# Result stores of the expert pairs issued by the sync engine instead of the scalar engine, from four result buffers

## The chip, the cores and the metric

The kernel runs on one core of a Trainium2 chip. The metric is device time in microseconds (us) of one execution. Five engines work beside each other and meet only at semaphores: TensorE (PE, matmuls and transposes into eight PSUM banks), VectorE (DVE), ScalarE (ACT), GpSimd (POOL) and the sync engine (SP). SP and ACT each issue DMAs into a queue of their own, q1 and q10 in the profile; sixteen DMA engines carry the packets of all queues.

## The reference

A block with attention, retention and a mixture of experts is followed by a second block of two layers. The change touches the experts alone. Of 64 experts every one of 512 tokens picks two; all is float32:

```python
def expert_block(args):
    xb, e = args
    hid = jax.nn.silu(xb @ w1[e]) * (xb @ w3[e])   # 1024 -> 512
    return hid @ w2[e]                             # 512 -> 1024

y_slots = lax.map(expert_block, (x_slots, blk_eid)).reshape(n_blocks * MOE_BLOCK, D)
y_assign = y_slots[dest].astype(jnp.float32) * s_gate[:, None]
return jax.ops.segment_sum(y_assign, s_tok, num_segments=T).astype(x2.dtype)
```

w1, w3 and w2 of an expert are 2 MB each, 403 MB in all; y_slots is an intermediate in DRAM.

## The kernel before

The kernel is a row of blocks: norm, mixer, merge, norm with the router's loads, the experts (`moe_block`), then `layers_block`, whose first work is to gather rows of `y_slots` with indirect DMAs. A block begins when all engines are through with the one before.

In `moe_block` each expert has 32 slots for tokens (CAP), and the experts go in pairs: 32 pairs, as eight iterations (`NIT`) of four pairs `pp`. Each engine runs its own loop over them.

*Weights.* A pair needs six loads of 2 MB, in the order w1, w3, w1, w3, w2, w2 (`PARTS`), each into one of eight slots `m.w` (`WSLOT`). `loads_of_router` issues the first eight ahead of the block. In `sp_moe`, SP then issues load x + 8 when the slot of load x is free: for the four up projection slots of a pair after `up_done`, for the two w2 slots after `down_done` (L1012 on). SP does nothing else here.

*PE* (`pair`): it waits for four loads, does the up projections of both experts into bank `pr` = pp % 2 (64 matmuls, L1068), raises `up_done`; for odd pairs it gathers the tokens of the next four experts (64 matmuls, L1053); then it waits for VectorE's `hid`, transposes it (L1077), waits for ACT's copy `ht`, for the two w2 loads, and for `yo_ready`, and does the down projection into bank 3 + pr (32 matmuls, L1087), `down_done`.

*ACT* (`act_moe`): Silu of the bank into `hs` (L1156), copy of gathered tokens for odd pairs (L1148), copy of the transposes (L1160). Then it waits for `yo_ready` and issues the store of the result (L1162): 128 partitions of 2 KB from `m.yo[pr]`, 256 KB, to `y_slots`, in a pattern whose outermost dimension is the half h of the columns, of size 2.

*VectorE* (`dve_moe`): the selection matrix for the next gather (L1293, L1310, L1315), the product `hid` (L1319), and the copy of the down projection from PSUM to `m.yo[pr]` (L1324), raising `yo_ready`. Before this copy it waits for `y_sent{pr}`, the store of the pair two before from the same buffer. In the order of VectorE's queue this copy stands ahead of the product of the next pair.

Semaphores y_sent0 and y_sent1 start at 16 (raised by ACT). At the end ACT waits for all stores. A last part for experts with more than 32 tokens (`sp.If(n > 0)`) follows on each engine.

Of the kernel before, what the change touches and what calls it, by code (L numbers as in the profile page):

```python
# [815 lines left out]
def merge_block(nc, m, G, banks, A):  # L816
    merge_memory(m)
    with nc.Block() as block:
# [81 lines left out]
        def _(pool):  # L900
# [8 lines left out]
CAP = 32  # L909
# [4 lines left out]
ROUTER_SEMS = ["rw_in", "logits_done", "logits_ready", "r_exp_in", "r_exp", "assigned", "counted",  # L914
               "routed", "zeroed", "eb_sent", "eb_in", "r_step"]
MOE_SEMS = ["up_done", "hs_ready", "hid_ready", "ht_turned", "ht_ready", "down_done", "yo_ready",
            "y_sent0", "y_sent1", "g_ready", "gather_done", "xt_ready", "g_step",
            "ov_in", "ov_g", "ov_gathered", "ov_xt", "ov_up", "ov_hs", "ov_hid", "ov_turned",
            "ov_ht", "ov_down", "ov_y", "ov_sent", "ov_step"] + [f"e_in{i}" for i in range(WSLOT)]
COMB_SEMS = [f"y_in{i}" for i in range(8)] + ["combined"]  # L920
# [2 lines left out]
def moe_memory(arena):  # L923
    m = persistent(arena)
    sp = Space(arena, m.free)
    m.hn = sp(T, D)
    m.rw = sp(KT, NG + NE)
    m.rb = sp(NG + NE)
    m.iota = sp(P)
    m.piota = sp(1)  # L930
    m.before, m.ones = sp(P), sp(P)
    m.lg = sp(T, NG + NE)
    m.r8 = [sp(T, 8) for _ in range(8)]
    m.r1 = [sp(T) for _ in range(12)]
    m.prod = sp(T, NG * GE)
    m.pick = [sp(T, NE) for _ in range(2)]
    m.both = sp(T, NE)
    m.pos = sp(T, NE)
    m.e64 = [sp(NE) for _ in range(5)]
    m.k8 = [sp(2, T) for _ in range(6)]  # L940
    m.yrel = sp(2, T)
    m.misc = sp(4)
    m.misc_i = sp(4).bitcast(i32)
    m.eb_i = sp(MORE).bitcast(i32)
    m.norm_at = sp.at
    m.G = sp(T, P)
    m.G1 = sp(T, P)
    m.xt = sp(KT, P)
    m.hs, m.hid = sp(FF), sp(FF)
    m.ht = sp(FF // P, 2 * CAP)  # L950
    m.yo = [sp(512) for _ in range(2)]
    at = sp.at
    m.w = [sp(KT * FF) for _ in range(WSLOT)]
    norm_views(m, m.norm_at)
    assert m.norm_smalls <= at
    return m
# [4 lines left out]
NGRP = NE // 4  # L961
# [17 lines left out]
def load_expert(sp, m, G, A, at, i):  # L979

    pp, j = at // 6, at % 6
    e = 8 * i + 2 * pp + (j // 2 if j < 4 else j - 4)
    sp.dma_start(m.w[at % WSLOT], expert_src(A, PARTS[j], e)).then_inc(G[f"e_in{at % WSLOT}"], 16)
# [16 lines left out]
        load_expert(sp, m, G, A, at, 0)  # L1000


def sp_moe(sp, m, G, A, eb_dram):
    sp.wait_ge(G["routed"], 1)
    sp.dma_start(eb_dram.rearrange("a b -> b a"), m.misc_i[0:MORE, 0:1]).then_inc(G["eb_sent"], 16)
    sp.wait_ge(G["eb_sent"], 16)
    sp.dma_start(m.eb_i[0:1, :], eb_dram).then_inc(G["eb_in"], 16)

    def loads(i, n):
        for x in range(n):  # L1010
            pp, j = x // 6, x % 6
            sp.wait_ge(G["up_done" if j < 4 else "down_done"], 4 * i + pp + 1)  # L1012
            load_expert(sp, m, G, A, x + WSLOT, i)

    with sp.Fori(0, NIT - 1) as i:
        loads(i, 24)
    loads(NIT - 1, 24 - WSLOT)
    sp.wait_ge(G["eb_in"], 16)
    n = sp.value_load(m.misc_i[0:1, 1:2], min_val=0, max_val=MORE - 1)
    with sp.If(n > 0):  # L1020
        sp.wait_ge(G["up_done"], NE // 2)
        sp.wait_ge(G["down_done"], NE // 2)
        with sp.Fori(0, n) as j:
            e = sp.value_load(m.eb_i[0:1, bass.ds(j, 1)], min_val=0, max_val=NE - 1)
            sp.wait_ge(G["ov_down"], j + 1)
            sp.dma_start(m.w[0], expert_src(A, "w1", e)).then_inc(G["ov_in"], 16)
            sp.dma_start(m.w[1], expert_src(A, "w3", e)).then_inc(G["ov_in"], 16)
            sp.dma_start(m.w[4], expert_src(A, "w2", e)).then_inc(G["ov_in"], 16)
# [105 lines left out]
def act_moe(act, m, G, banks, y_slots):  # L1134
    turned = banks[2][:, :].rearrange("p (f c) -> p f c", f=FF // P)
    act.wait_ge(G["r_exp_in"], 1)
    act.activation(m.r8[1], m.r8[0], ACT.Exp).then_inc(G["r_exp"], 1)
    act.wait_ge(G["r_exp_in"], 2)
    act.activation(m.r1[3], m.r1[2], ACT.Exp).then_inc(G["r_exp"], 1)

    act.sem_inc(G["y_sent0"], 16)
    act.sem_inc(G["y_sent1"], 16)
    act.sem_inc(G["ov_sent"], 16)

    def xt_copy(n):
        for d in range(2):
            act.wait_ge(G["gather_done"], n + d + 1)
            act.activation(m.xt[:, 4 * d:4 * d + 4, :],  # L1148
                           banks[5 + d][:, :].rearrange("p (a c) -> p a c", a=4), ACT.Copy)\
               .then_inc(G["xt_ready"], 1)  # L1150

    def experts(i, last):
        for pp in range(4):
            h, pr = pp // 2, pp % 2
            act.wait_ge(G["up_done"], 4 * i + pp + 1)
            act.activation(m.hs[64:128, :], banks[pr][0:64, :], ACT.Silu).then_inc(G["hs_ready"], 1)  # L1156
            if pr and not (last and h):
                xt_copy(4 * i + 2 * h + 2)
            act.wait_ge(G["ht_turned"], 4 * i + pp + 1)
            act.activation(m.ht, turned[:, :, 0:2 * CAP], ACT.Copy).then_inc(G["ht_ready"], 1)  # L1160
            act.wait_ge(G["yo_ready"], 4 * i + pp + 3)
            act.dma_start(y_slots[bass.ds(8 * CAP * i + 2 * CAP * pp, 2 * CAP), :]  # L1162
                          .rearrange("r (h c) -> h r c", h=2), m.yo[pr])\
               .then_inc(G[f"y_sent{pr}"], 16)

    xt_copy(0)
    with act.Fori(0, NIT - 1) as i:
        experts(i, False)
    experts(NIT - 1, True)
    act.wait_ge(G["y_sent0"], 16 * NGRP + 16)  # L1170
    act.wait_ge(G["y_sent1"], 16 * NGRP + 16)
    act.wait_ge(G["routed"], 1)
    n = act.value_load(m.misc_i[0:1, 1:2], min_val=0, max_val=MORE - 1)
    with act.If(n > 0):
        with act.Fori(0, n) as j:
            act.wait_ge(G["ov_gathered"], j + 1)
            act.activation(m.xt[:, :, 0:CAP],
                           banks[5][:, 0:KT * CAP].rearrange("p (a c) -> p a c", a=KT), ACT.Copy)\
               .then_inc(G["ov_xt"], 1)
            act.wait_ge(G["ov_up"], j + 1)  # L1180
            act.activation(m.hs[64:64 + CAP, :], banks[0][0:CAP, :], ACT.Silu).then_inc(G["ov_hs"], 1)
            act.wait_ge(G["ov_turned"], j + 1)
            act.activation(m.ht[:, :, 0:CAP],
                           turned[:, :, 0:CAP], ACT.Copy)\
               .then_inc(G["ov_ht"], 1)
            act.wait_ge(G["ov_y"], j + 1)
            act.dma_start(y_slots[bass.ds(CAP * (j + MAIN), CAP), :].rearrange("s (h c) -> h s c", h=2),
                          m.yo[0][0:64, :]).then_inc(G["ov_sent"], 16)
            act.wait_ge(G["ov_sent"], 16 * j + 32)
# [8 lines left out]
def dve_moe(dve, m, G, banks):  # L1198
# [107 lines left out]
    def experts(i, last):  # L1306
        for h in range(2):
            g = 2 * i + h
            dve.wait_ge(G["g_ready"], g + 1)
            dve.tensor_scalar(m.yrel, m.yrel, -float(P), None, ALU.add).then_inc(G["g_step"], 1)  # L1310
            dve.wait_ge(G["g_step"], 3 * g + 3)
            if not (last and h):
                dve.wait_ge(G["gather_done"], 2 * g + 2)
                picks(P, 3 * g + 3)
                dve.tensor_tensor(m.G, m.G, m.G1, ALU.add).then_inc(G["g_ready"], 1)  # L1315
            for pr in range(2):
                n = 4 * i + 2 * h + pr
                dve.wait_ge(G["hs_ready"], n + 1)
                dve.tensor_tensor(by_place(m.hid[0:64, :], FF // P), spread(banks[pr][64:128, :], FF // P),  # L1319
                                  spread(m.hs[64:128, :], FF // P), ALU.mult)\  # L1320
                   .then_inc(G["hid_ready"], 1)
                dve.wait_ge(G["down_done"], n + 1)
                dve.wait_ge(G[f"y_sent{pr}"], 16 * g + 16)
                dve.tensor_copy(m.yo[pr], banks[3 + pr][:, :]).then_inc(G["yo_ready"], 1)  # L1324

    dve.wait_ge(G["zeroed"], 1)
    with dve.Fori(0, NIT - 1) as i:
# [3 lines left out]
    n = dve.value_load(m.misc_i[0:1, 1:2], min_val=0, max_val=MORE - 1)  # L1331
    with dve.If(n > 0):
        dve.wait_ge(G["gather_done"], 2 * NGRP)
        dve.wait_ge(G["y_sent0"], 16 * NGRP + 16)
        dve.sem_inc(G["ov_step"], 1)
        with dve.Fori(0, n) as j:
            dve.wait_ge(G["ov_step"], j + 1)
# [13 lines left out]
def moe_block(nc, m, G, banks, A, eb_dram, y_slots, cleared):  # L1351

    with nc.Block() as block:

        @block.sync
        def _(sp):
            sp_moe(sp, m, G, A, eb_dram)

        @block.tensor
        def _(pe):  # L1360
            pe_moe(pe, m, G, banks)

        @block.scalar
        def _(act):
            act_moe(act, m, G, banks, y_slots)

        @block.gpsimd
        def _(pool):
            pool_moe(pool, m, G, cleared)

        @block.vector
        def _(dve):
            dve_moe(dve, m, G, banks)
# [1241 lines left out]
```

## Time and profile before

| | us |
|---|---|
| median of three runs | 3670.3 (3670.26 to 3672.96) |
| the profiled execution | 3671.4 |
| its span, first to last instruction | 3669.6 |
| PE busy, of the span | 2984.2 (81%) |
| VectorE, ScalarE, GpSimd busy | 673.6, 489.9, 254.9 |

The expert pairs take the span from about 1074 to 2143 us. A row for a group of instructions gives line, engine and operation, output <- input, shape and count, then busy us, mean ns of one, then the idle time of the engine ahead of them and what ended it. "arena" is the one tile that holds all of SBUF. A row of a timeline gives the start and the length in us, then the instruction, and in brackets the idle time before it. SPq and ACTq are issues of DMAs by these engines; their length is the issue, not the transfer. The share of the DMA engines is a mean over sixteen. The span stands 1.8 us below the execution's time, which stands 1.1 us above the median.

### The profile page before, as it was taken

To read this page: it belongs to the slowest core of one execution; us is meant where nothing else is said; L and a number is where in the kernel's file an instruction comes from. 1 tells how busy PE (TensorE), PEld (TensorE's weight loads), DVE (VectorE), ACT (ScalarE), POOL (GpSimd) and SP (SyncE) were. 2 spreads that over 40 slices of the span, in tenths; PEclk is the share of its full clock that TensorE was granted. 3 is DMA by queue.
4 is the path that set the end of the run, shared out by engine and by line. 5 is a ranking of instruction groups with operands and counts; after the bars stand their busy time and mean duration, and the time that the engine had idled before them with its cause. 6 is when DMAs were issued, how large, how long until landed. Compare 5 with 4: busy or idle time off the path is not lost. (4 is left out here: it accounts for less than half of the span.)

```text
span 3669.6 us, 29297 instructions
## 1 busy us (share of the span) xinstructions
PE 2984.2 (81%) x12116; PEld 1559.9 (43%) x12116; DVE 673.6 (18%) x1777; ACT 489.9 (13%) x954; POOL 254.9 (7%) x247
## 2 busy tenths in 40 slices
PE   6999999999865455454455449999999999999999
PEld 4666666544642122122122126444444464444443
DVE  1222222210130000100100032332220123321102
ACT  1222232210010000000000021310000113110000
POOL 1000002210000000000000030020000110110000
PEclk9999999999977777787777679899999998999999
DMA  6211111112179998898889841112221211122220
GB/s 199 52 35 52 35 35 52 46 46 92 55 302 428 379 381 345 378 393 358 378 365 393 355 174 71 58 46 69 80 92 69 71 60 68 41 74 80 78 83 35
DMA packets 192664, 587.39 MB, mean 160 GB/s; under 512 B 16434, under 2 KB 142642, under 8 KB 167730
## 3 DMA queue, kind: packets, MB, share of 16 engines
q1 hardware_dynamic: 186210, 569.19, 40.3%
q10 hardware_dynamic: 4160, 8.39, 0.6%
q0 software_dynamic: 2192, 8.39, 0.6%
q8 instruction: 72, 1.18, 0.1%
q14 instruction: 30, 0.25, 0.0%
HBM read 571.26 MB, written 14.68 MB: 160 GB/s over the span
## 5 line engine op out<-in xcount | busy, mean ns | idle before, releaser
L2310 PE MATMUL bank<-arena 128*128 128x512 f32 (+2 forms) x1472 | 608.9, 576 | 9.1 <-DVE arena L1675 9.1
L1068 PE MATMUL bank<-arena 128*32 128x512 f32 x2048 | 264.5, 674 | 224.2 <-DMA arena<-in_moe_w 223.1
L330 PE MATMUL bank<-arena 128*128 128x384 f32 x1280 | 430.9, 489 | 14.3 <-DMA arena<-in_w_in 14.3
L2310 PEld LDWEIGHTS bank<-arena 128*128 128x128 f32 x1472 | 276.0, 191 | 340.1 <-issue 330.1
L330 PEld LDWEIGHTS bank<-arena 128*128 128x128 f32 x1280 | 237.4, 190 | 175.1 <-DMA arena<-in_w_in 14.5
L2319 PE MATMUL bank<-arena 128*128 128x512 f32 x704 | 303.2, 592 | 0.0
L1077 PE MATMUL bank<-arena 128*128 128x128 f32 x128 | 28.8, 366 | 280.6 <-DVE arena L1319 280.6
L1790 PE MATMUL bank<-arena 128*128 128x512 f32 (+3 forms) x736 | 250.2, 498 | 0.0
L1068 PEld LDWEIGHTS bank<-arena 128*32 128x32 f32 x2048 | 75.4, 122 | 411.0 <-issue 411.0
L2319 PEld LDWEIGHTS bank<-arena 128*128 128x128 f32 x704 | 133.1, 189 | 168.4 <-issue 168.4
L1790 PEld LDWEIGHTS bank<-arena 128*128 128x128 f32 x736 | 138.3, 190 | 101.2 <-issue 69.5
L1324 DVE COPY arena<-bank 128x512 f32<-128x512 f32 x32 | 22.2, 693 | 804.8 <-DMA y_slots<-arena 753.4
L1087 PE MATMUL bank<-arena 128*32 128x512 f32 x1024 | 145.2, 718 | 16.9 <-ACT arena L1160 16.9
L1077 PEld LDWEIGHTS bank<-arena 128*128 128x128 f32 x128 | 19.1, 183 | 297.4 <-DVE arena L1319 297.4
L1053 PE MATMUL bank<-arena 128*128 128x128 f32 x1024 | 119.9, 278 | 16.3 <-DVE arena L1299 16.3
L1053 PEld LDWEIGHTS bank<-arena 128*128 128x128 f32 x1024 | 116.9, 193 | 29.1 <-DVE arena L1299 16.5
L1156 ACT ACTIVATE arena<-bank 64x512 f32<-64x512 f32 x32 | 18.9, 591 | 742.5 <-DVE arena L1324 481.0
L1977 PE MATMUL bank<-arena 128*128 128x512 f32 x256 | 111.6, 592 | 1.4 <-ACT arena L2076 1.4
L327 PE MATMUL bank<-arena 128*128 128x512 f32 x256 | 110.9, 593 | 0.0
L2361 DVE TENSOR_SCALAR arena<-arena 128x512 f32<-128x512 f32 x44 | 25.3, 575 | 457.9 <-ACT arena L2347 457.9
L2347 ACT ACTIVATE arena<-bank 128x512 f32<-128x512 f32 x44 | 26.3, 598 | 522.9 <-PE bank L2310 522.9
L391 PE MATMUL bank<-arena 128*128 128x64 f32 x640 | 81.0, 275 | 12.3 <-ACT arena L455 12.3
(299 smaller groups left out, 2571.7 us busy)
## 6 DMA issues: line engine op xcount, KB each, us to landing
arena<-in_moe_w SPq DMA_DIRECT2D x192, 2048.0 KB, 24.4
arena<-in_w_up SPq DMA_DIRECT2D x44, 1024.0 KB, 7.7
arena<-in_w_in SPq DMA_DIRECT2D x52, 512.0 KB, 5.7
arena<-in_w_down SPq DMA_DIRECT2D x10, 2048.0 KB, 7.7
arena<-in_w_in SPq DMA_DIRECT2D x12, 1024.0 KB, 5.2
y_slots<-arena ACTq DMA_DIRECT2D x32, 256.0 KB
arena<-in_w_in SPq DMA_DIRECT2D x4, 2048.0 KB, 9.5
arena<-in_w_out SPq DMA_DIRECT2D x4, 2048.0 KB, 8.2
```

The source lines that it names most:

```text
L327: ins = pe.matmul(banks[s % 2][:, :], w[:, k, tile(b)], m.aT[:, k, :], start=(k == 0), stop=(k == KT - 1))
L330: ins = pe.matmul(banks[s % 2][:, 0:CW], m.aT[:, k, tile(t)], w[:, k, :], start=(k == 0), stop=(k == KT - 1))
L391: ins = pe.matmul(banks[2][:, 256:256 + HD], m.pt[:, tile(4 * i + j)], m.v[q % 2][:, k, g, HD * hh:HD * hh + HD], start=(i == 0 and j == 0 ...
L1053: ins = pe.matmul(banks[5 + d // 4][:, tile(d % 4)], m.hn[:, t, tile(d)], m.G[:, t, :], start=(t == 0), stop=(t == T - 1))
L1068: ins = pe.matmul(banks[pr][q:q + CAP, :], m.xt[:, k, c:c + CAP], up_view(m, slots[2 * e2 + up])[:, k, :], start=(k == 0), stop=(k == KT - 1))
L1077: ins = pe.transpose(banks[2][:, tile(f)], m.hid[:, tile(f)], m.ident)
L1087: ins = pe.matmul(banks[3 + pr][q:q + CAP, :], m.ht[:, f, CAP * e2:CAP * e2 + CAP], down_view(m, slots[4 + e2])[:, f, 512 * half:512 * hal ...
L1790: ins = pe.matmul(out, a, b, start=(i == 0), stop=(i == len(terms) - 1))
L1977: ins = pe.matmul(row_banks(banks, 2 * l + 1, t)[half][:, :], m.mixT[:, k, tile(t)], slot_view(m, i)[:, k, :], start=(first and k == ks[0] ...
L2310: ins = pe.matmul(banks[2 * (j % 2) + half][:, part], w[:, k, c0:c0 + P], m.aT[:, k, part], start=(k == 0), stop=(k == KT - 1))
L2319: ins = pe.matmul(banks[2 * t + half][:, :], m.hidT[:, k, tile(t)], v[:, k % 4, 512 * half:512 * half + 512], start=(k == 0), stop=(k == N ...
L2347: act.activation(m.gp[j % 2][:, 2:], banks[2 * (j % 2) + 1][:, :], ACT.Copy).then_inc(G["f_gcopy"], 1)
```

## The change

SP issues the 32 stores: `store` waits for `yo_ready` of its pair and issues the same transfer into SP's queue, right after the last load that follows `down_done` of this pair. In the last iteration the stores of its pairs 2 and 3 come after all loads. ACT no longer waits for `yo_ready` nor issues stores in the pairs. There are four result buffers `m.yo` instead of two, two of them over tiles of the router that are no longer used, and four semaphores y_sent; the copy of a pair waits for the store of the pair four before. At the end SP and ACT both wait for all stores.

```diff
+    m.yo = [sp(512) for _ in range(2)] + [Space(arena, at + 512 * i)(512) for i in range(2)]
@@ sp_moe
+    for n in range(4):
+        sp.sem_inc(G[f"y_sent{n}"], 16)
     ...
             sp.wait_ge(G["up_done" if j < 4 else "down_done"], 4 * i + pp + 1)
             load_expert(sp, m, G, A, x + WSLOT, i)
+            if j == 5:
+                store(i, pp)
+
+    def store(i, pp):
+        sp.wait_ge(G["yo_ready"], 4 * i + pp + 3)
+        sp.dma_start(y_slots[bass.ds(8 * CAP * i + 2 * CAP * pp, 2 * CAP), :]
+                     .rearrange("r (h c) -> h r c", h=2), m.yo[pp]).then_inc(G[f"y_sent{pp}"], 16)
 
     with sp.Fori(0, NIT - 1) as i:
         loads(i, 24)
     loads(NIT - 1, 24 - WSLOT)
+    store(NIT - 1, 2)
+    store(NIT - 1, 3)
+    for n in range(4):
+        sp.wait_ge(G[f"y_sent{n}"], 16 * NIT + 16)
@@ act_moe
-            act.wait_ge(G["yo_ready"], 4 * i + pp + 3)
-            act.dma_start(y_slots[bass.ds(8 * CAP * i + 2 * CAP * pp, 2 * CAP), :]
-                          .rearrange("r (h c) -> h r c", h=2), m.yo[pr])\
-               .then_inc(G[f"y_sent{pr}"], 16)
@@ dve_moe
                 dve.wait_ge(G["down_done"], n + 1)
-                dve.wait_ge(G[f"y_sent{pr}"], 16 * g + 16)
-                dve.tensor_copy(m.yo[pr], banks[3 + pr][:, :]).then_inc(G["yo_ready"], 1)
+                dve.wait_ge(G[f"y_sent{2 * h + pr}"], 16 * i + 16)
+                dve.tensor_copy(m.yo[2 * h + pr], banks[3 + pr][:, :]).then_inc(G["yo_ready"], 1)
```

## Rows read from the trace of the kernel before

**Rows 1.** Costliest groups of the page: up projection, transposes, copy of the result.
```profile
L1068 PE MATMUL bank<-arena 128*32 128x512 f32 x2048 | 264.5, 674 | 224.2 <-DMA arena<-in_moe_w 223.1
...
L1077 PE MATMUL bank<-arena 128*128 128x128 f32 x128 | 28.8, 366 | 280.6 <-DVE arena L1319 280.6
...
L1324 DVE COPY arena<-bank 128x512 f32<-128x512 f32 x32 | 22.2, 693 | 804.8 <-DMA y_slots<-arena 753.4
```
**Rows 2.** Timeline of VectorE, the copies of the results of two pairs in a row.
```profile
1410.90 0.69 DVE L1324 COPY arena<-bank 128x512 f32<-128x512 f32 x1 [36.72 <-DMA y_slots<-arena]
...
1451.34 0.69 DVE L1324 COPY arena<-bank 128x512 f32<-128x512 f32 x1 [36.33 <-DMA y_slots<-arena]
```
**Rows 3.** Waits of SP from 1075 to 2144 us: total, times, longest.
```profile
SPq L983 <- PE bank L1087: 481.4, 30, 32.8
SPq L983 <- PE bank L1068: 439.3, 30, 26.2
```
**Rows 4.** DMA queues and issues, 1075.6 to 2133.2 us: packets, MB, share; KB each.
```profile
q1 hardware_dynamic: 26490, 385.79, 86.7%
q10 hardware_dynamic: 4029, 8.13, 2.0%
...
arena<-in_moe_w SPq DMA_DIRECT2D x182, 2048.0 KB, 24.5
y_slots<-arena ACTq DMA_DIRECT2D x31, 256.0 KB
```
**Rows 5.** Engines by windows; the last two columns are DMA share and GB/s.
```profile
core 0: us, PE busy (x) PEld busy (x) DVE busy (x) ACT busy (x) POOL busy (x), PEclk, DMA share, GB/s
...
1530.00:1560.00 30.00, 13.44 (x100) 3.96 (x92) 1.03 (x1) 0.98 (x2) 0.00 (x0) 0.73 1.01 429
1493.50:1503.50 10.00, 6.15 (x44) 2.14 (x48) 2.54 (x4) 2.26 (x3) 0.00 (x0) 0.65 0.13 51
...
2037.50:2048.00 10.50, 7.59 (x44) 2.33 (x48) 2.31 (x3) 0.98 (x2) 0.00 (x0) 0.56 0.14 57
2124.00:2132.00 8.00, 5.15 (x24) 1.71 (x28) 1.10 (x2) 0.98 (x2) 0.00 (x0) 0.58 0.14 53
2133.30:2135.50 2.20, 0.30 (x4) 0.00 (x0) 0.69 (x1) 0.00 (x0) 0.00 (x0) 1.00 0.00 0
```
**Rows 6.** DMA queues, 2124 to 2132 us, after the last load: packets, MB, share.
```profile
q10 hardware_dynamic: 202, 0.41, 13.1%
```
**Rows 7.** The same from 1300 to 1340 us, among loads.
```profile
q10 hardware_dynamic: 129, 0.26, 1.7%
```
**Rows 8.** Instructions that write y_slots: ns min/median/max of an issue, first and last start.
```profile
L1162 ACTq DMA_DIRECT2D y_slots<-arena x32: 522/530/1199, 1083.5 to 2134.4; - x32
```
**Rows 9.** Timeline of PE, up projections of two pairs and a gather.
```profile
1387.85 8.80 PE L1068 MATMUL bank<-arena 128*32 128x512 f32 x64 [7.49 <-DMA arena<-in_moe_w]
...
1421.50 7.09 PE L1068 MATMUL bank<-arena 128*32 128x512 f32 x64
1428.52 7.41 PE L1053 MATMUL bank<-arena 128*128 128x128 f32 x64
```
**Rows 10.** Timeline of all engines, the last pair and the start of the next block.
```profile
2113.53 7.05 PE L1068 MATMUL bank<-arena 128*32 128x512 f32 x64
2123.38 0.69 DVE L1324 COPY arena<-bank 128x512 f32<-128x512 f32 x1 [16.39 <-DMA y_slots<-arena]
...
2124.67 0.59 ACT L1156 ACTIVATE arena<-bank 64x512 f32<-64x512 f32 x1 [16.08 <-DVE arena L1324]
2125.29 1.03 DVE L1319 TENSOR_TENSOR arena<-bank,arena 64x512 f32<-64x512 f32 x1 [1.22 <-ACT arena L1156]
...
2133.68 0.69 DVE L1324 COPY arena<-bank 128x512 f32<-128x512 f32 x1 [7.36 <-PE bank L1087]
2134.41 0.52 ACTq L1162 DMA_DIRECT2D y_slots<-arena  x1
2143.43 0.34 SPq L2374 DMA_DIRECT2D arena<-in_norm_final_w  x1
```

More of the change, by code:

```diff
@@ L916 @@
 MOE_SEMS = ["up_done", "hs_ready", "hid_ready", "ht_turned", "ht_ready", "down_done", "yo_ready",
-            "y_sent0", "y_sent1", "g_ready", "gather_done", "xt_ready", "g_step",
+            "y_sent0", "y_sent1", "y_sent2", "y_sent3", "g_ready", "gather_done", "xt_ready", "g_step",
             "ov_in", "ov_g", "ov_gathered", "ov_xt", "ov_up", "ov_hs", "ov_hid", "ov_turned",
@@ L934, in moe_memory @@
     m.r1 = [sp(T) for _ in range(12)]
+    at = sp.at
     m.prod = sp(T, NG * GE)
@@ L950, in moe_memory @@
     m.ht = sp(FF // P, 2 * CAP)
-    m.yo = [sp(512) for _ in range(2)]
+    assert sp.at >= at + 1024
+    m.yo = [sp(512) for _ in range(2)] + [Space(arena, at + 512 * i)(512) for i in range(2)]
     at = sp.at
@@ L1000, in loads_of_router, with sp_moe @@
         load_expert(sp, m, G, A, at, 0)
-def sp_moe(sp, m, G, A, eb_dram):
+def sp_moe(sp, m, G, A, eb_dram, y_slots):
+    for n in range(4):
+        sp.sem_inc(G[f"y_sent{n}"], 16)
     sp.wait_ge(G["routed"], 1)
@@ L1139, in act_moe @@
     act.activation(m.r1[3], m.r1[2], ACT.Exp).then_inc(G["r_exp"], 1)
-    act.sem_inc(G["y_sent0"], 16)
-    act.sem_inc(G["y_sent1"], 16)
     act.sem_inc(G["ov_sent"], 16)
@@ L1169, in act_moe @@
     experts(NIT - 1, True)
-    act.wait_ge(G["y_sent0"], 16 * NGRP + 16)
-    act.wait_ge(G["y_sent1"], 16 * NGRP + 16)
+    for n in range(4):
+        act.wait_ge(G[f"y_sent{n}"], 16 * NIT + 16)
     act.wait_ge(G["routed"], 1)
@@ L1333, in dve_moe @@
         dve.wait_ge(G["gather_done"], 2 * NGRP)
-        dve.wait_ge(G["y_sent0"], 16 * NGRP + 16)
+        dve.wait_ge(G["y_sent0"], 16 * NIT + 16)
         dve.sem_inc(G["ov_step"], 1)
@@ L1356, in _ @@
         def _(sp):
-            sp_moe(sp, m, G, A, eb_dram)
+            sp_moe(sp, m, G, A, eb_dram, y_slots)
         @block.tensor
```

## Prediction

> **What bounds the kernel now.** I read the costliest groups first, and of those the lines of the expert pairs. TensorE is the engine at work, yet it stands still for 224.2 us ahead of the up projections (L1068), for weights, and for 280.6 us ahead of the transposes (L1077), for VectorE's product; VectorE in turn stands for 753.4 us ahead of the copy of the result (L1324), for the store of an earlier result [rows 1]. It looks as if the stores set the pace: two copies in a row lie 40.4 us apart, each at the end of a wait of over 36 us [rows 2]. The sync engine waits all the time for TensorE to free slots, 481.4 and 439.3 us [rows 3], so its queue has room.
>
> The next view says otherwise. The DMA queues from 1075.6 to 2133.2 us carried 385.79 MB of weights (q1) and 8.13 MB of results (q10, 31 stores) in 1057.6 us [rows 4], a share of 88.7% of sixteen engines, not 100. But what do the sixteen engines do when weights are short? In 1493.5:1503.5 and in 2037.5:2048, between two bursts of loads, the share is 0.13 and 0.14 and the rate 51 and 57 GB/s: two engines of sixteen (0.125), each at some 26 GB/s; the same at 2124:2132, where stores alone run [rows 5]. A store is 130 packets, 128 of 2 KB and two small ones (4029 for 31) [rows 4]. **Every store runs on the same two engines**, 65 packets each, and the loads use all sixteen; I take the reason to be the outermost dimension of the store's pattern, the h of size 2.
>
> So I add up the work of those two. A load: where all sixteen are full (1530:1560, share 1.01) they move 429 GB/s [rows 5]; 2.097 MB / 429 GB/s = 4.89 us. A store: 202 packets in 8.0 us on two engines [rows 6] is 0.079 us a packet, times 65 = 5.15 us. The stretch holds 184 loads and 31 stores: 184 x 4.89 + 31 x 5.15 = 899.8 + 159.7 = **1059.5 us against 1057.6 us measured**. In bytes: 385.79/16 + 8.13/2 = 28.18 MB for each of the two, 26.6 GB/s against 26.8 when full. These two engines never rest in the whole stage; they are the bound. The 36 us waits of VectorE are what a consumer shows that has been given a longer queue than it can hold: while loads run, a store has 129 packets in 40 us [rows 7], which is one store packet for each load packet on its two engines (64 result packets on each of the two in 40 us leave 40 - 64 x 0.079 = 34.9 us, or 7.1 loads at 4.89 us, of 9 packets each there). It is thus slow without costing more.
>
> **The change part by part.**
> Removed from ScalarE: 32 store issues of 0.53 us [rows 8], 17 us, and the wait for yo_ready ahead of them. ScalarE's work of a pair is three or four short copies, and it waits for the same copy of VectorE; worth nothing by itself.
>
> Removed from VectorE: with four buffers the copy of pair n waits for the store of pair n-4. The new store stands behind at most the six loads already issued, so it lands some 6 x 4.89 + 5.15 = 34.5 us after its issue, and four pairs take 138 us. The 753.4 us go. What is late next is the load: TensorE's wait at L1077 turns into wait at L1068, one for one, since the weights come no sooner.
>
> Added to the sync engine: a wait for yo_ready after each pair's last load, one issue of about 0.53 us and register work, 32 times, some 17 us beside 921 us of waiting [rows 3]. Queued behind that wait are the four loads that wait for up_done of the next pair. The copy follows down_done by a semaphore and takes 0.7 us; up_done of the next pair comes after another 64 matmuls, 7.1 to 8.8 us [rows 9]. The loads are never held.
>
> Moved in the DMA queue: the stores leave the queue of their own and stand in the one queue in order of issue. The two engines then do 48 weight packets (six loads) and 64 result packets per pair in turn: period 6 x 4.89 + 5.15 = 34.5 us. Do they ever run dry? When a pair's fourth load lands, four more loads and one store are queued, 24.7 us; the up projection takes at most 8.8 us [rows 9], and then four loads are added with 15.9 us still in the queue. With gather (7.4 us), transposes, copies and down projection the pair is through some 24 us after that landing, before the next pair's weights at 34.5 us. Dry time: none. Cost of a store among loads: rows show 5.15 us in both forms, alone and interleaved. What no row shows is loads and stores taking turns in one queue. Lower end 0: taking turns between two queues, packet by packet, costs nothing by the sum above, and back to back stores with their closing packets run without a hole (202 packets fill the 8 us, 13.1% of 16 engines, i.e. two at work all the time [rows 6]). A gain below zero has no source, as the bytes of the two engines stay. Upper end: a store that starts on an idle queue moves nothing for at least 1.1 us (issue 2134.41, share 0.00 up to 2135.5), and from issue to the next block takes 9.0 us, 3.9 more than its packets [rows 5, 10]; 31 x 3.9 = 121 us if each store among loads showed all that. I take 0, since the rows nearest to it (mixed work, and a full queue) show none.
>
> The Trainium skill, page "DMA: Bandwidth & Descriptors", section "Anatomy of one DMA", speaks against this change: it gives each DMA a fixed cost of about 2 us, mostly the wait until the last byte is confirmed, longest where the target is HBM. It is described there for another issue path. If a shared queue stood still for it, 31 x 2 = 62 us would come on top by that page, an estimate. The back to back stores above show the closing packet passing without such a hole, so I do not follow it.
>
> The tail is where the order matters. Before, the two engines were through with 184 loads and 31 stores at 2133.2 us, the stores trailing. After, the same work ends at the same time, but all loads come ahead of store 31 (the next to last), so the last load lands at 2133.2 - 5.15 = 2128.1 us and the last w3 of the up projections two loads earlier, 2118.3 us. Up projection after idling 8.8 us: 2127.1; 0.2 to ScalarE, then 9.0 us from Silu to the copy as now (2124.67 to 2133.68): 2136.3 us, against 2133.68 now [rows 9, 10]. In the kernel before that pair had its matmuls begun at 2113.53, but then waited for the store until 2123.38 [rows 10]. Net +2.6 us (+0.9 if the matmuls find the faster clock and take 7.1 us). The last store starts on an idle queue in both.
>
> **Sum**: stage 0, tail +2.6 us. The profiled execution took 3671.4 us (span 3669.6), so 3674.0 us; the median of the three runs is 1.1 us lower, so **3673.0 us**. A measurement of this kernel can tell about 0.2%, 7.3 us, from no change; this is inside.
>
> **Rivals.** *A, slower: the turn between loads and stores in one queue costs.* If the two engines drain the loads before the first result packet, and the store before the next load, each store costs a hole. At the 1.1 us of an idle start: 31 x 1.1 = 34 us, 3670.3 + 34 + 3 = 3707 us; at 3.9 us, 3794 us. It decides from 7.3 / 31 = 0.24 us a store. For it: a mixed single queue is not in the trace. Against: above. 0.10.
> *B, slower: the queue of the two engines runs dry* because loads are asked for late behind the sync engine's new wait; it takes over 15.9 us of delay in a pair, from where each further us costs 31 us: at 1 us 3704 us. Nothing in the rows is near. 0.03.
> *C, faster: VectorE's wait was the bound.* Then the stretches of 0.13 share were lost load time, and with the copies free the loads run full: down to 184 x 4.89 for the stage, 3670.3 - 158 = 3512 us, if a store also came to use all sixteen engines from this queue; if the stores keep two engines, nothing. It falls with the sum of 1059.5 against 1057.6 us. 0.05, part of it for a gain of 10 to 30 us from a better mix.
> *D: the change doesn't do what it says*, the wait for the stores returns with four buffers. That takes a landing of over 138 us; the time is again the bound's, 3673 us. It is inside the forecast.
>
> **How the numbers follow.** No change by more than 7.3 us: 0.79 (forecast, with D). Slower: A 0.10, B 0.03, 0.01 for a tail worse than worked out. Faster: C 0.05, 0.02 for a few us gained in the tail. Range 3663 us (just over 7 us below the median, the limit of the middle case) to 3684 us (which takes in A up to (3684 - 3673) / 31 = 0.35 us a store).
>
> **What would show it.** L1324 no longer waits for y_slots; L1077's idle time falls to a few tens of us and L1068's wait for weights rises to about 450 us; the queue q10 is gone. Pairs run at an even 34.5 us. The share of the DMA engines stays near 0.89 over the stage, which ends within 3 us of where it did. Wrong would be: a stage over 1067 us with the two engines not full, holes at the stores' ends (A), a burst of loads asked for with nothing queued (B), or the stage shorter by over 7 us (C).

## The result and the profile after

| | before | changed |
|---|---|---|
| median, us | 3671.6 (3669.6 to 3674.3, 8 runs) | 3683.2 (3681.8 to 3687.4, 8 runs) |
| ratio | | 1.0030, 95% interval 1.0020 to 1.0039 |
| two more comparisons | 3673.3; 3673.2 | 3683.1, 1.0029 (1.0019 to 1.0039); 3682.6, 1.0024 (1.0014 to 1.0034) |
| span of the profiled execution | 3669.6 | 3685.6 |
| first load that SP issues in the stage | 1074.46 | 1082.10 |
| first issue of the next block | 2143.43 | 2159.52 |
| the stage between these two | 1069.0 | 1077.4 |

The change costs 9 to 12 us, 0.3%. That is just more than the 0.2% that a measurement of this kernel can tell from no change, so it is a small loss and not the "no change" of the forecast. The range 3663 to 3684 holds it.

Rows of the changed kernel: the two lines of TensorE on which the waiting was seen before, VectorE's copy of the result (out of a window over the stage), and the one queue that is left of the two. Columns as in [rows 1].

```profile
L1083 PE MATMUL bank<-arena 128*32 128x512 f32 x2048 | 294.0, 737 | 488.3 <-DMA arena<-in_moe_w 487.3
...
L1092 PE MATMUL bank<-arena 128*128 128x128 f32 x128 | 20.2, 280 | 30.1 <-DVE arena L1328 30.1
L1333 DVE COPY arena<-bank 128x512 f32<-128x512 f32 x32 | 22.2, 693 | 240.6 <-PE bank L1102 240.6
...
q1 hardware_dynamic: 190370, 577.58, 40.7%
```

Against [rows 1]: the 753 us for which VectorE stood before its copy (now L1333) have gone from the stores; TensorE's wait for VectorE's product (now L1092) fell from 281 to 30 us, and its wait for weights (now L1083) rose from 224 to 488 us. The sum of the two was 505 us and is 518 us. VectorE's wait for stores, the most striking of the profile, was removed in full; on TensorE 250 us less of waiting for the product came back as 264 us more of waiting for the weights.

Where do the 16 us between the two profiled spans lie? 8.4 us lie in the stage. 7.6 us lie ahead of it, in instructions that the change does not touch. Windows over the router's logits, first the kernel before, then the changed one (columns as in [rows 5]):

```profile
1018.00:1026.00 8.00, 7.33 (x64) 7.22 (x64) 1.12 (x5) 1.28 (x1) 0.53 (x1) 1.00 1.02 432
```
```profile
1018.00:1026.00 8.00, 8.00 (x39) 8.00 (x40) 0.47 (x2) 1.25 (x1) 0.49 (x1) 0.52 1.01 430
1026.00:1034.00 8.00, 5.58 (x27) 5.38 (x26) 2.22 (x10) 0.23 (x1) 0.00 (x0) 0.50 1.01 434
```

The same 64 matmuls took 7.33 us at a granted clock of 1.00 (2.4 GHz) and 13.58 us at 0.52 and then 0.50 (1.2 GHz), 6.25 us more. The same split runs through eleven traces of the kernels in this document: in six the first load of the stage lies at 1074.5 to 1077.1 us and these matmuls have a granted clock of 1.00; in five it lies at 1080.4 to 1082.1 us and they have 0.50 to 0.58. All three traces of the changed kernel are among the five, but so are two of kernels whose stores ScalarE issues, while four kernels whose stores the sync engine issues and that differ from the changed one in the store or its buffers alone are among the six. So I count it as chance, which three traces of the changed kernel do not prove. The stage's own 8.4 us are what the change is shown to cost; the medians lie 9.4 to 11.6 us apart.

**In the stage**, the DMA traffic and its end. The queues of the changed kernel from 1083.2 to 2147.9 us, then two windows at the end, where the next to last store runs alone on two engines and where nothing runs but an instruction fetch, then the timeline of the last pair:

```profile
q1 hardware_dynamic: 30519, 393.92, 88.2%
...
arena<-in_moe_w SPq DMA_DIRECT2D x182, 2048.0 KB, 23.3
y_slots<-arena SPq DMA_DIRECT2D x31, 256.0 KB
```
```profile
2143.00:2147.60 4.60, 2.62 (x24) 1.10 (x28) 1.03 (x1) 0.78 (x2) 0.00 (x0) 1.00 0.13 50
2147.90:2151.00 3.10, 1.38 (x16) 0.17 (x8) 0.69 (x1) 0.00 (x0) 0.00 (x0) 1.00 0.02 5
```
```profile
2133.46 9.28 PE L1083 MATMUL bank<-arena 128*32 128x512 f32 x64 [18.60 <-DMA arena<-in_moe_w]
2142.80 0.59 ACT L1169 ACTIVATE arena<-bank 64x512 f32<-64x512 f32 x1 [31.64 <-PE bank L1083]
...
2149.35 0.69 DVE L1333 COPY arena<-bank 128x512 f32<-128x512 f32 x1 [4.90 <-PE bank L1102]
2150.07 0.51 SPq L1023 DMA_DIRECT2D y_slots<-arena  x1
2159.52 0.35 SPq L2383 DMA_DIRECT2D arena<-in_norm_final_w  x1
```

The same 184 loads and 31 stores that took the two busiest DMA engines 1057.6 us [rows 4] took 1064.7 us here: 7.1 of the 8.4 us. The rest, 1.4 us, is the tail: 11.6 us from there to the next block against 2143.43 - 2133.2 = 10.2 us.

What is new in this trace is the length of the sync engine's load issues. Rows of the instructions that write the weights (min/median/max in ns), before and changed:

```profile
L983 SPq DMA_DIRECT2D arena<-in_moe_w x192: 328/380/785, 1010.7 to 2090.9; - x192
```
```profile
L985 SPq DMA_DIRECT2D arena<-in_moe_w x192: 327/608/7326, 1010.0 to 2115.9; - x192
```

Once a pair, the first load after a store is held at its issue for 4 to 7.3 us. And some loads land late: by the landing times in the trace (when a transfer's semaphore is full), loads follow each other at 4.89 us and with a store between them at 9.9 to 10.0 us, but nine gaps of 5.26 to 5.87 us stand among them, 6.2 us over 4.89 in sum. The first of the nine, 5.87 us in the first pair, has its like in every trace (6.00 us in the kernel before). The other eight, two in every eight pairs, are new with the change: 5.2 us in sum.

### The profile page after: what moved, and what is told of

It reads as the page before. It is cut to its first block and busy times, and to the rows that moved or that the text cites. A ratio compares the mean times of both kernels' runs of the same rounds, so it can differ in the third digit from the quotient of the medians.

```text
span 3685.6 us, 29318 instructions
## 1 busy us (share of the span) xinstructions
PE 2984.9 (81%) x12116; PEld 1563.1 (42%) x12116; DVE 674.4 (18%) x1777; ACT 489.9 (13%) x954; POOL 256.5 (7%) x247
## 5 line engine op out<-in xcount | busy, mean ns | idle before, releaser
L1083 PE MATMUL bank<-arena 128*32 128x512 f32 x2048 | 294.0, 737 | 488.3 <-DMA arena<-in_moe_w 487.3
L2319 PEld LDWEIGHTS bank<-arena 128*128 128x128 f32 x1472 | 275.9, 191 | 340.2 <-issue 330.4
L1083 PEld LDWEIGHTS bank<-arena 128*32 128x32 f32 x2048 | 81.6, 132 | 700.0 <-issue 700.0
L330 PEld LDWEIGHTS bank<-arena 128*128 128x128 f32 x1280 | 237.1, 190 | 174.9 <-DMA arena<-in_w_in 14.5
L2328 PEld LDWEIGHTS bank<-arena 128*128 128x128 f32 x704 | 133.0, 189 | 168.4 <-issue 168.4
L1799 PEld LDWEIGHTS bank<-arena 128*128 128x128 f32 x736 | 138.4, 190 | 101.3 <-issue 69.6
L1328 DVE TENSOR_TENSOR arena<-bank,arena 64x512 f32<-64x512 f32 x32 | 33.3, 1042 | 744.9 <-ACT arena L1169 744.9
L1068 PE MATMUL bank<-arena 128*128 128x128 f32 x1024 | 121.4, 280 | 16.3 <-DVE arena L1308 16.3
L1068 PEld LDWEIGHTS bank<-arena 128*128 128x128 f32 x1024 | 118.4, 195 | 29.1 <-DVE arena L1308 16.5
L2433 POOL DMA_INDIRECT arena<-y_slots,arena x8 | 8.1, 1015 | 1143.9 <-POOLq L1362 1141.8
L1706 DVE SCALAR_TENSOR_TENSOR arena<-arena,bank 128x512 f32<-128x512 f32 x32 | 21.8, 687 | 356.4 <-PE bank L2328 270.0
```

What stands on the lines that cost most here:

```text
L330: ins = pe.matmul(banks[s % 2][:, 0:CW], m.aT[:, k, tile(t)], w[:, k, :], start=(k == 0), stop=(k == KT - 1))
L1068: ins = pe.matmul(banks[5 + d // 4][:, tile(d % 4)], m.hn[:, t, tile(d)], m.G[:, t, :], start=(t == 0), stop=(t == T - 1))
L1083: ins = pe.matmul(banks[pr][q:q + CAP, :], m.xt[:, k, c:c + CAP], up_view(m, slots[2 * e2 + up])[:, k, :], start=(k == 0), stop=(k == KT - 1))
L1799: ins = pe.matmul(out, a, b, start=(i == 0), stop=(i == len(terms) - 1))
L2319: ins = pe.matmul(banks[2 * (j % 2) + half][:, part], w[:, k, c0:c0 + P], m.aT[:, k, part], start=(k == 0), stop=(k == KT - 1))
L2328: ins = pe.matmul(banks[2 * t + half][:, :], m.hidT[:, k, tile(t)], v[:, k % 4, 512 * half:512 * half + 512], start=(k == 0), stop=(k == N ...
```

## The experiments

Two theories at the start. **Theory 1**: two of sixteen DMA engines carry all stores besides their share of the loads and are the bound of the stage; the loss comes from how stores and loads share their queue. **The rivals**: VectorE's waits cost time; the buffers cost it; or the number of engines has nothing to do with it.

### The queue and the buffers, each alone

The changed kernel again, as the measure.

> The changed kernel itself once more, as the measure for its neighbours. In its trace the two DMA engines that carry the stores work from 1083.1 to 2147.9 us, 1064.8 us for the same bytes that took 1057.7 us before; the next block starts 8.4 us later counted from the first load of the stage, and 7.6 us lie ahead of that load, in code that the change does not touch. Theory 1 (the stage costs 8.4 us, what lies ahead is chance): 3680 us or 9 us over the kernel before, and the stage again 1077 us from first load to next block. Theory 2 (the change also shifts what lies ahead): again some 7 us ahead of the first load, 12 us or more in all.

Measured 3683.1 us (1.0029, 1.0019 to 1.0039); stage 1077.5 us; first load at 1081.87 us. 9.8 us over the kernel before: the stage's part is steady, and of what lies ahead the trace has 7.4 us again.

Buffers alone:

```diff
-    m.yo = [sp(512) for _ in range(2)]
+    m.yo = [sp(512) for _ in range(2)] + [Space(arena, at + 512 * i)(512) for i in range(2)]
 ... four semaphores y_sent; ACT issues as before, from m.yo[pp], with y_sent{pp}
-                dve.wait_ge(G[f"y_sent{pr}"], 16 * g + 16)
+                dve.wait_ge(G[f"y_sent{2 * h + pr}"], 16 * i + 16)
```

> The buffers alone: ScalarE issues the stores into its own queue as before, from four buffers. Theory 1 (two DMA engines are the bound, and their work is the same while stores and loads sit in two queues): VectorE's wait of 753 us shrinks, TensorE's wait for weights grows to about 480 us, and the two engines still need 1057 to 1058 us for 184 loads and 31 stores; the tail is up to 4 us shorter since the last copy is done before the stores that are still queued. 3667 us, within 1 us of that or equal to the kernel before. Rival (VectorE's waits cost time): 20 us or more faster. Rival (four buffers let stores collide with loads, and that is what made the changed kernel slower): 3680 us.

Measured 3671.3 us, 0.9996 (0.9987 to 1.0005), equal to the kernel before and not 4 us below it. The one execution of this run that has a trace took 17400 us, for a cause that is not known, while the eleven others took 3667.6 to 3674.4; so the trace is of a second run:

> The kernel with four buffers and ScalarE's own queue once more, for its trace; its time lay at 3671.3 us beside 3673.3 of the kernel before. Theory (the two DMA engines are the bound and their work costs less in two queues than in one): VectorE's wait for stores well below 753 us, TensorE's wait for weights about 480 us as in the changed kernel, and from the first load to the next block 1065 to 1069 us, where the changed kernel took 1077. Issues of loads take 0.4 us throughout, none of the 4 to 7 us of the changed kernel. Rival (the changed kernel loses its time in the order of the last pairs, not in the queue): the pairs' pace is 34.3 us here too and only the tail is shorter.

Measured 3670.1 us, 0.9991 (0.9981 to 1.0001), and a stage of 1064.6 us (1077.11 to 2141.72). Time and stage are as expected; the way to them is not. TensorE waited 249 us for weights, not 480, and 252 us for VectorE's product, and VectorE for ScalarE. ScalarE was held at its store issues. Its row for them, and three in a row from its timeline:

```profile
L1164 ACTq DMA_DIRECT2D y_slots<-arena x32: 522/10668/51094, 1084.5 to 2131.5; - x32
```
```profile
1379.42 30.74 ACTq L1164 DMA_DIRECT2D y_slots<-arena  x1
1419.42 29.86 ACTq L1164 DMA_DIRECT2D y_slots<-arena  x1
1459.36 30.00 ACTq L1164 DMA_DIRECT2D y_slots<-arena  x1
```

Four buffers let VectorE go on, but here the queue does not take a third store while two are in it; ScalarE stands for 30 us where VectorE stood before, with the same pace of 40 us. The rival that the buffers cost time falls. The one that VectorE's wait costs time is not tested by this run, since the wait only moved: a wait that bounds a stage could move as well and leave the time as it is. What speaks against that rival is the changed kernel, where no engine waits for a store until the last pair is through and the stage is still 8.4 us longer.

Queue alone:

```diff
-                     .rearrange("r (h c) -> h r c", h=2), m.yo[pp]).then_inc(G[f"y_sent{pp}"], 16)
+                     .rearrange("r (h c) -> h r c", h=2), m.yo[pp % 2]).then_inc(G[f"y_sent{pp % 2}"], 16)
 ... and VectorE waits for the store two pairs before, as in the kernel before
```

> The queue alone: the sync engine issues the stores as in the changed kernel, but from two buffers. Theory 1 (the single queue costs the 7 us: result packets stand back to back at 0.080 us instead of 0.0757 us between load packets, about 4 us in all, and issues held for 4 to 7 us make the other fourteen engines start in bursts, about 3 us): no wait of VectorE, as a store lands within 35 us of its issue and the buffer is needed 69 us later, so the same time as the changed kernel to 1 us, 3680 to 3683 us. Rival (the buffers cost it): 3671 us.

Measured 3685.0 us, 1.0028 (1.0019 to 1.0038), 2 us above both the changed kernel and the forecast. The stage took 1081.0 us, 3.6 us more than in the changed kernel. After the first pair thirteen loads land late instead of eight, 8.9 us in sum instead of 5.2, which is about this difference. No wait of VectorE for a store is left with two buffers either. So the loss comes with the single queue; two more buffers show no effect on ScalarE's queue and at most a gain of some 2 us on the sync engine's.

### Stores over sixteen engines

```diff
-        sp.dma_start(y_slots[bass.ds(8 * CAP * i + 2 * CAP * pp, 2 * CAP), :]
-                     .rearrange("r (h c) -> h r c", h=2), m.yo[pp]).then_inc(G[f"y_sent{pp}"], 16)
+        for h in range(2):
+            sp.dma_start(y_slots[bass.ds(8 * CAP * i + 2 * CAP * pp, 2 * CAP), 512 * h:512 * h + 512],
+                         m.yo[pp][64 * h:64 * h + 64, :]).then_inc(G[f"y_sent{pp}"], 16)
 ... counts of y_sent doubled
```

> The changed kernel with each store issued as two transfers of 64 rows, one for each half of the columns, so that the outermost dimension is 64 instead of 2. Theory 1 (the store runs on two of sixteen engines because of that 2, and these two are the bound): each half spreads over sixteen engines, a store costs each engine 8 packets, 0.64 us, instead of 5.05; a pair takes 6 x 4.89 + 0.7 = 30.0 us instead of 34.4, 31 x 4.4 = 136 us less: 3547 us. TensorE is not yet the bound: its work of a pair is some 24 us. The issues of loads behind a store are no longer held. Rival (the number of engines has nothing to do with it, two more issues per pair cost a little): 3683 us or more. Rival (HBM bandwidth bounds the sum of loads and stores): at most 20 us less.

Measured **3540.3 us, 0.9643 (0.9629 to 0.9658)**, 143 us below the changed kernel, stage 936.0 us. The bytes, the packets of 2 KB and the queue are the same; each store is two transfers of 64 rows, and the outermost dimension of their pattern is 64 instead of 2. Engines by windows, 700 us in the middle of the stage, and the issue row of its loads:

```profile
1200.00:1900.00 700.00, 398.63 (x3072) 177.57 (x3076) 65.95 (x94) 41.90 (x75) 0.00 (x0) 0.80 1.01 428
...
L985 SPq DMA_DIRECT2D arena<-in_moe_w x192: 327/379/782, 1010.1 to 1969.8; - x192
```

The share of all sixteen engines is 1.01 throughout, where the changed kernel has 0.89 from 1200 to 2100 us. By the landing times a store adds 0.63 us to a load instead of 5.05. No issue of a load is held, and after the first pair no load lands late. The 143 us are 31 x (5.07 - 0.63) = 138 us and the 5 us of the late loads. The same on the other queue, from the kernel before with its two buffers:

```diff
-            act.dma_start(y_slots[bass.ds(8 * CAP * i + 2 * CAP * pp, 2 * CAP), :]
-                          .rearrange("r (h c) -> h r c", h=2), m.yo[pr])\
-               .then_inc(G[f"y_sent{pr}"], 16)
+            for c in range(2):
+                act.dma_start(y_slots[bass.ds(8 * CAP * i + 2 * CAP * pp, 2 * CAP), 512 * c:512 * c + 512],
+                              m.yo[pr][64 * c:64 * c + 64, :]).then_inc(G[f"y_sent{pr}"], 16)
 ... counts of y_sent doubled
```

> The kernel before (ScalarE issues, two buffers) with each store issued as two transfers of 64 rows, which spread over sixteen DMA engines. Theory (spread stores leave nothing that queue or buffers could change: a store costs each engine 0.63 us and lands within some 6 us of load packets, long before its buffer is needed): the same as with the sync engine's queue and four buffers, 3540 us to 3 us; VectorE's wait for stores is gone with two buffers. Rival (two buffers are too few whatever the engines): 3600 us or more.

Measured **3542.2 us, 0.9640 (0.9624 to 0.9656)**; stage 935.2 us. No wait for a store is among VectorE's waits. This is an edit of a few lines on the kernel before, and it is 3.6% faster than that and 3.8% faster than the changed kernel; queue and number of buffers are then of no matter. That a store used two engines, and that these were the bound, is shown by this pair of runs with the shares of 0.13 and 1.01.

### Every result stored twice

```diff
+        for y in (y_slots, Y_AGAIN):
+            sp.dma_start(y[bass.ds(8 * CAP * i + 2 * CAP * pp, 2 * CAP), :]
+                         .rearrange("r (h c) -> h r c", h=2), m.yo[pp]).then_inc(G[f"y_sent{pp}"], 16)
 ... in place of the one store; y_again is a second tensor in DRAM; counts of y_sent doubled
```

> The changed kernel with every result stored twice, the second time to another place in DRAM (this adds work; the output does not change). Theory 1 (two engines are the bound): each of 32 further stores costs its full 5.05 us though nobody waits for it, 3683 + 160 = 3843 us, pairs at 39.4 us. Rival (a store is hidden behind loads): 3683 us to 5 us.

Measured 3833.0 us, 1.0437 (1.0420 to 1.0454). 150 us more for 32 stores for which nobody waits, 4.7 us each: the dose as well as its removal follows the two engines. But it was 10 us less than expected. The trace tells of a part of it: loads land 4.89 us apart, and 15.02 us apart with two stores between them, so a store costs 5.07 us, and there are *no late loads* after the first pair, which is 5 us less. The stage takes 1229.7 us.

> The kernel with four buffers on ScalarE's queue, every result stored twice, the second time to another place in DRAM (adds work). Theory 1a (the single queue costs a fixed amount per store, by result packets that stand back to back and by load issues that are held): 32 further stores at 4.92 us, 3671 + 157 = 3828 us, and the distance to the sync engine's version with double stores grows from 12 to 18 to 24 us. Theory 1b (the distance is not per store but comes from the tail and from starts in bursts that happen once in eight pairs): the distance stays 9 to 13 us, 3832 us. VectorE waits again here, as a store pair takes 80 us among loads; it costs nothing by either.

Measured 3833.8 us, 1.0435 (1.0417 to 1.0452); stage 1229.3 us. That is 163.7 us over the run with four buffers and single stores, 5.1 us for each further store. The distance between the queues is 0 here, neither 18 to 24 us nor 9 to 13 us. Both versions of my theory fall: if the single queue costs a fixed amount per store, these runs do not show it. With the late loads gone on one side, and a longer rest of stores after the last load on the other (36.8 us from there to the next block against 22.0 us), the two queues come out equal.

### The place of the store in the queue

```diff
             load_expert(sp, m, G, A, x + WSLOT, i)
-            if j == 5:
-                store(i, pp)
+            if j == 3 and pp:
+                store(i, pp - 1)
+            elif j == 3 and prev is not None:
+                store(prev, 3)
 ... prev is the iteration before; its last pair's store is issued in the next one
```

> The changed kernel, but the sync engine issues the store of a pair after the four up projection loads of the next pair instead of ahead of them; queue, buffers and bytes are the same. In the changed kernel the first load after a store is held at its issue for 4 to 7 us, the fourteen engines without stores run out of work meanwhile, and nine loads land 0.3 to 1.0 us late, 6 us in all, twice in eight pairs. Theory 2 (the held issues cause these): with fewer packets waiting when the store is issued no load is held as long, the late landings go, and the last store also starts 3 us sooner, as all loads come ahead of two stores: 3674 us, the two engines at 5.1 us a store instead of 5.3. Theory 3 (each change between loads and stores in one queue costs 0.2 us): only the tail's 3 us, 3680 us, pairs at 34.4 us as before. Rival (the store's place in the queue is of no matter at all, tail included): 3683 us.

Measured 3680.4 us, 1.0019 (1.0010 to 1.0028); stage 1073.0 us. Beside it on the same chip:

> The changed kernel beside the former, on the same chip, as its measure: 3683 us, 1077 us from the first load of the stage to the next block, held issues and late landings at the same pairs as in its other two traces.

Measured 3682.6 us, 1.0024 (1.0014 to 1.0034); stage 1076.5 us; nine late loads as in the other traces, the eight after the first pair at the same places. The store's later place gained 2.2 us by the medians, 3.5 us by the stages, which is the tail: all loads come ahead of two stores. The held issues did not become shorter but longer, as the first window of the sync engine's timeline shows (six issues that took 24 us in sum, most of it the first), while in the changed kernel six issues and a hold take 10 us:

```profile
1243.26 24.09 SPq L985 DMA_DIRECT2D arena<-in_moe_w  x6
1267.99 0.56 SPq L1025 DMA_DIRECT2D y_slots<-arena  x1
```
```profile
1415.73 10.01 SPq L985 DMA_DIRECT2D arena<-in_moe_w  x6
1425.99 0.83 SPq L1023 DMA_DIRECT2D y_slots<-arena  x1
```

The late loads stayed, nine after the first pair, in the same rhythm of eight pairs. So theory 2 was not tested as meant (its condition, shorter holds, did not come about), but a hold three times as long changed neither the number nor the size of the late loads by much. Theory 3, 0.2 us for each turn between loads and stores, had the time right (3680), but it does not fit the double stores: they take as many turns, and two stores add 10.13 us where one adds 5.07, which leaves nothing for the turn.

## Why the prediction was right, and where it was short

*The bound: right.* The step from the waits of VectorE [rows 1, 2] to the two engines of [rows 5] carried the forecast. It was put to the test from both sides: 143 us less with the stores spread (136 us had been forecast from 4.89 and 0.64 us), and 150 us more with the stores doubled. Rival C, that VectorE's wait was the bound, falls with it. The time that C named for stores on all sixteen engines, 3512 us, came near once they were there (3540 us), but by the store's pattern and not by the change.

*The wait turns into wait for weights, one for one: right.* 281 us at the transposes became 30, and 224 us at the up projections became 488; "a few tens" and "about 450" had been said. The copies run at the pace forecast: 1601.32, 1669.91 and 1738.55 us are two pairs apart each, 34.3 us a pair against 34.5.

*The sync engine's wait for yo_ready holds no loads: right* (its one wait there, 31.6 us, is for the last store), *but "the loads are never held" was wrong*: the queue holds them, 4 to 7.3 us once a pair. During such a hold the share falls to 0.11 and 0.12 (1245.5 to 1246.5 and 1211 to 1213.5 us), so the other fourteen engines run dry while the two still have packets. So rival B, that the two run dry, did not come about.

*Stage 0: the term that failed*, by 7.1 us in the profiled execution. I had bounded a store among loads by [rows 6] and the sum of [rows 4] and took 0 for the price of sharing one queue. What the runs showed in its place is, for the most part, late loads: the eight of the changed kernel after the first pair make 5.2 of the 7.1 us. They are in all three of its traces and in those with the queue alone and with the later store, and not in those with spread or doubled stores. With the queue alone they are more, and the stage is longer by about as much.

The other 1.9 us are 0.06 us a store. One source was argued: while two queues are served in turn, loads land 5.57 us apart on average and a store is through every 40.3 us, which is 40.3 x (1 - 4.89 / 5.57) = 4.92 us a store, and in one queue it is 5.05 to 5.07. That would be 4 us over the stage. But the whole stage of the kernel before comes to (1057.6 - 899.8) / 31 = 5.09 us a store, small delays of its own included, and the doubled stores show no difference between the queues. So a price per store is not shown, and the 1.9 us stay unexplained. By the landing times the prediction's 5.15 us a store were 0.08 to 0.10 us too many. Rival A had this place, but not this mechanism: it had put the limit of no change at 0.24 us a store, and 7.1 / 31 = 0.23 us is what came.

*The tail, +2.6 us: the right sign, 1.4 us measured.* The last pair's matmuls began 14.4 us ahead of the end of the two engines' work (forecast 14.9), took 9.28 us (8.8), but from Silu to the copy it was 6.55 us instead of 9.0. The transposes and the down projection took 0.66 and 3.64 us, at a granted clock of 1.00; in the kernel before they took 1.11 and 5.64 us, at 0.58 [rows 5]. That is 2.45 us, the whole difference. The forecast took the row of the kernel before, where TensorE had stood still for 5.8 us just before them; here it was 1.8 us.

*The chances.* "No change by over 0.2%" had 0.79 and "slower" 0.14. The measured ratio of 1.0024 to 1.0030 is just on the slower side, and the loss of 9 to 12 us is some four times the forecast's 2.6. That 3683.2 us lies in the range, by 0.8 us, is in part luck. So is the right sign, since it was forecast from the tail alone and the tail brought 1.4 us. The prediction's own sign, a stage that ends within 3 us of where it did, did not come: 8.4 us. A forecast of 3673 us with a price of 0 sat at the lower bound of a price that could hardly be below 0; the middle of what was possible lay above it.

**What stays open.** What makes eight loads land late, twice in eight pairs, when stores and loads share a queue. Holds at the issue are not enough: with doubled stores loads are held for up to 6.5 us and the second store of a pair for 29 us, and no load lands late. No run forces the late loads or takes them away with the stores left as they are. Open too is whether the clock ahead of the stage has to do with the change.

## What to carry to other kernels

When the engines wait for a transfer, ask which of the sixteen DMA engines carry it before asking which engine issues it: a share of 0.13 with work still in the queue is two engines, and their sum of work is the bound, whatever the mean share of 0.89 says. Look at the outermost dimension of such a transfer, here 64 instead of 2 for 3.6%, before moving it to another queue or adding buffers. A long wait can be a symptom: when it is removed and the same time comes back as another wait, for weights here, the bound lies behind both. A wait that only moves to another engine proves nothing.

## What the runs showed of the hardware that I had not expected

- *An issue is held while much is queued.* With 2 KB packets on two engines, ScalarE's third store stood for 30 us at its issue while two stores (65 packets an engine each) were in the queue, and SP's loads stood 4 to 7.3 us behind a store, up to 25 us with the store placed later. The same loads take 0.38 us at the median otherwise, and at most 0.79 us in the kernel before and with spread stores. How much the queue takes was not measured.
- *Two queues with work are served packet by packet in turn.* One 2 KB packet passed for each 16 KB packet, so a 256 KB store took 40 us among loads and 5.1 us alone, at nearly the same cost to the engine. In the kernel before, from 1301.00 to 1302.38 us, the queue of the stores moved four packets, one for each of the two engines in every 0.69 us, which is one load packet (0.61 us) and one result packet (0.08 us).

```profile
q10 hardware_dynamic: 4, 0.01, 1.5%
```

The Trainium skill, page "DMA: Bandwidth & Descriptors", section "Queues, rings and completion order", lets an engine stay with one queue for some 9 to 17 descriptors before it turns to the other. The 40 us alone would fit that too, at nine for nine; by it, result packets would come in runs of nine or more with nothing for 4.9 us between. The trace shows one at a time here.

- *The store's pattern decides the number of engines.* With an outermost dimension of 2 a store ran on two engines (share 0.13), with two transfers of 64 on sixteen (0.63 us on each). The Trainium skill, page "DMA: Bandwidth & Descriptors", section "Why a DMA increments its semaphore by 16 and not by 1", takes the largest number up to 16 that divides the outermost sizes of both sides, and by it 2 gives two and 64 gives sixteen. The two runs with spread stores agree.
- *The end of a store leaves no hole of 2 us in the queue.* The 2 us per transfer weighed in the prediction would have been 62 us; 7 came, and double stores, with twice as many ends, show 5.07 us each.
